# Delta-rule stage: the first level's mask, moved from Pool to the vector engine

## What is computed

```
kb = kc * bc[..., None]
a_mat = jnp.where(tril_strict, jnp.einsum('bhnid,bhnjd->bhnij', kb, kc) * decay, 0.0)
l_mat = a_mat + jnp.eye(CHUNK, dtype=a_mat.dtype)
u = lax.linalg.triangular_solve(l_mat, vc * bc[..., None], left_side=True, lower=True, unit_diagonal=True)
w = lax.linalg.triangular_solve(l_mat, kb * jnp.exp(gc)[..., None], left_side=True, lower=True, unit_diagonal=True)
...
def step(state, inp):
    a_i, qd_i, kt_i, u_i, w_i, gl_i = inp
    v_new = u_i - jnp.einsum('bhck,bhkv->bhcv', w_i, state)
    o_i = jnp.einsum('bhck,bhkv->bhcv', qd_i, state) + jnp.einsum('bhij,bhjv->bhiv', a_i, v_new)
    state = state * gl_i[..., None, None] + jnp.einsum('bhck,bhcv->bhkv', kt_i, v_new)
    return state, o_i
```

## Time and profile before

| | |
|---|---|
| median of 3 runs | 1487.34 us (1486.9 to 1489.47) |
| the profiled execution's own time | 1485.48 us |
| its span | 1483.6 us |
| mean granted TensorE clock | 0.997 |
| busy: PE | 1438.0 us (97%) |
| busy: DVE | 801.7 us (54%) |
| busy: ACT | 619.0 us (42%) |
| busy: Pool | 425.0 us (29%) |
| delta stage | about 1119 to 1245 us of the span |

### The profile page before, as it was taken

One profiled execution on the slowest core, in us unless ns is written; L12 is line 12 of the kernel. 1 busy time (PEld: TensorE's weight loads), 2 busy tenths in 40 slices (PEclk: granted clock), 3 DMA queues, 4 the chain that ended last, 5 costly groups with the idle time before them and its releaser, 6 DMA issues.

```text
span 1483.6 us, 30802 instructions
## 1 busy us (share of the span) xinstructions
PE 1438.0 (97%) x12682; PEld 1267.8 (85%) x12682; DVE 801.7 (54%) x1474; ACT 619.0 (42%) x1249; POOL 425.0 (29%) x527
## 2 busy tenths in 40 slices
PE   6999999989999999999999999999998998999998
PEld 6999998867777778878899999888897886888887
DVE  5238410149999878735420723452424776888431
ACT  5322121027777677632432113332325554777210
POOL 0212132110000277623202212221205884434320
PEclk9999999999999999999999999999999999999999
DMA  8313222000000043256325244433121021222342
GB/s 261 55 51 104 87 92 70 27 1 1 1 1 1 17 130 105 66 177 171 92 43 59 50 94 85 59 59 56 29 68 41 28 90 44 61 76 71 100 131 82
DMA packets 88017, 105.32 MB, mean 71 GB/s; under 512 B 25343, under 2 KB 72095, under 8 KB 87880
## 3 DMA queue, kind: packets, MB, share of 16 engines
q1 hardware_dynamic: 87880, 103.36, 27.0%
HBM read 80.20 MB, written 23.12 MB: 70 GB/s over the span
## 4 chain that ended last, share of the span: by engine, by line
PE 56%; DVE 4%; ACT 2%; DMA 1%; issue 1%; SPq 0%; POOL 0%; DVEq 0%; ACTq 0%
PE ps L368 22%; PE ps L1336 12%; PE ps L2810 2%; PE ps L1144 2%; PE ps L1128 2%; PE ps L2796 2%; PE ps L2785 1%; PE ps L2215 1%; PE ps L2158 1%; PE ps L2173 1%; DMA p_w_raw<-w_in 1%; PE ps L2773 1%; PE ps L1123 1%; PE ps L1122 1%; PE ps L2786 1%
## 5 line engine op out<-in xcount | busy, mean ns | idle before, releaser
L334 POOL TENSOR_TENSOR p_w_lo<-p_w_raw,p_w_hi 128x2048 fp32r<-128x2048 f32 (+1 forms) x27 | 127.3, 4716 | 506.9 <-ACT p_w_hi L318 506.9
L368 PE MATMUL ps<-p_w_hi,w_out_hi 128*128 128x256 f32 (+1 forms) x640 | 181.9, 284 | 0.4 <-ACT p_spill L393 0.3
L368 PE MATMUL ps<-p_w_hi,w_out_lo 128*128 128x256 f32 (+1 forms) x640 | 179.7, 281 | 0.0
L368 PE MATMUL ps<-p_w_lo,w_out_hi 128*128 128x256 f32 (+1 forms) x640 | 179.6, 281 | 0.0
L368 PE MATMUL ps<-p_w_hi,hT_hi 128*128 128x256 f32 x576 | 163.7, 284 | 1.9 <-DVE hT_lo L140 1.9
L368 PE MATMUL ps<-p_w_hi,hT_lo 128*128 128x256 f32 x576 | 162.7, 282 | 0.0
L368 PE MATMUL ps<-p_w_lo,hT_hi 128*128 128x256 f32 x576 | 162.6, 282 | 0.0
L368 PEld LDWEIGHTS ps<-p_w_hi,w_out_hi 128*128 128x128 f32 x640 | 120.5, 188 | 1.5 <-ACT p_spill L393 0.8
L368 PEld LDWEIGHTS ps<-p_w_lo,w_out_hi 128*128 128x128 f32 x640 | 120.8, 189 | 0.0
L368 PEld LDWEIGHTS ps<-p_w_hi,w_out_lo 128*128 128x128 f32 x640 | 120.6, 188 | 0.0
L368 PEld LDWEIGHTS ps<-p_w_hi,hT_hi 128*128 128x128 f32 x576 | 109.0, 189 | 2.3 <-DVE hT_lo L140 2.3
(11 more groups left out here) (299 smaller groups left out, 3585.0 us busy)
## 6 DMA issues: line engine op xcount, KB each, us to landing
p_w_raw<-w_in SPq DMA_DIRECT2D x26, 1024.0 KB, 8.0
s_gate<-p_spill SPq DMA_DIRECT2D x48, 128.0 KB, 1.8
kbT<-x SPq DMA_DIRECT2D x8, 512.0 KB, 6.9
b_w_raw<-w_out SPq DMA_DIRECT2D x8, 512.0 KB, 6.2
qT<-s_gate SPq DMA_DIRECT2D x8, 512.0 KB, 6.9
qT<-x SPq DMA_DIRECT2D x8, 512.0 KB, 3.5
s_x<-qT SPq DMA_DIRECT2D x8, 512.0 KB, 3.1
c_table<-s_line SPq DMA_DIRECT2D x8, 512.0 KB, 3.6
```

The lines of the kernel that those rows point to most:

```text
L334: ops.tensor_tensor(self.w_lo[:, c % 2, :, 0:w], self.raw[:, :, 0:w], self.w_hi[:, c % 2, :, 0:w].bitcast(F32), ALU.subtract).then_inc(sel ...
L368: last = self.nc.tensor.matmul(out, lhs, rhs, start=(kt == 0 and i == 0), stop=(kt == KT - 1 and i == 2))
```

## The change

DVE now multiplies A with the mask of level 0 itself, straight into T, waits for that result, and subtracts T from the identity in place. Pool's mask of level 0 falls away and with it a wait on `T0_ready`. `level_masked` now counts five masks a tile and `T0_ready` two steps a tile, and the waits are renumbered. `Al` keeps its size, its level 0 is no longer written.

```
@@ -2151,7 +2151,7 @@
                 pe.wait_ge(s["X0_ready"], t + 1)
                 if l >= 2:
                     pe.wait_ge(s["X_ready"], m)
-                pe.wait_ge(s["level_masked"], LEVELS * t + l + 1)
+                pe.wait_ge(s["level_masked"], (LEVELS - 1) * t + l)
@@ -2297,17 +2297,20 @@
                 if t >= 1:
-                    dve.wait_ge(s["level_masked"], LEVELS * t)
+                    dve.wait_ge(s["level_masked"], (LEVELS - 1) * t)
                 nc.vector.tensor_tensor(A[:, :, :], own(2), dec[:, 0, :, :], ALU.mult).then_inc(s["A_ready"], 1)
 
             @staticmethod
             def attn(t):
-                dve.wait_ge(s["level_masked"], LEVELS * t + 1)
+                dve.wait_ge(s["A_ready"], t + 1)
+                nc.vector.tensor_tensor(T[:, t % 2, :, :], A[:, :, :],
+                                        levels[:, 0, :].unsqueeze(1).to_broadcast([P, H4, CHUNK]), ALU.mult).then_inc(s["T0_ready"], 1)
+                dve.wait_ge(s["T0_ready"], 2 * t + 1)
                 nc.vector.tensor_tensor(T[:, t % 2, :, :], levels[:, LEVELS + 1, :].unsqueeze(1).to_broadcast([P, H4, CHUNK]),
-                                        Al[:, t % 2, 0, :, :], ALU.subtract).then_inc(s["T0_ready"], 1)
+                                        T[:, t % 2, :, :], ALU.subtract).then_inc(s["T0_ready"], 1)
                 if t >= 2:
                     dve.wait_ge(s["uw_ready"], 2 * (t - 1))
-                dve.wait_ge(s["T0_ready"], t + 1)
+                dve.wait_ge(s["T0_ready"], 2 * t + 2)
                 nc.vector.transpose(blocks(X[:, t % 2]), blocks(T[:, t % 2])).then_inc(s["X0_ready"], 1)
@@ -2545,8 +2548,6 @@
                 pool.wait_ge(s["A_ready"], t + 1)
                 if t >= 2:
                     pool.wait_ge(s["Z_ready"], (LEVELS - 1) * (t - 1))
-                    pool.wait_ge(s["T0_ready"], t - 1)
-                mask_levels(t, 0, 1)
```

## The result

| | before | after |
|---|---|---|
| median (6 runs each) | 1487.59 us | 1493.57 us |
| range | 1486.63 to 1489.47 | 1492.34 to 1496.1 |
| ratio | | 1.0036, 95% interval 1.0026 to 1.0047 |
| span of the profiled execution | 1483.6 us | 1490.0 us |
| profiled execution's own time | 1485.48 us | 1492.34 us |

What follows compares the result with a forecast made beforehand. DVE's queue, not PE, was taken to bound a 4.2 us piece of each settled turn. 5.3 + 0.5 - 0.1 = +5.7 us on 1485.48 gave 1491.2, plus 1.9 for the median: 1493.0 us, range 1489.8 to 1496.1.

Steps and rivals of the forecast that it cites:

- six settled turns: Delta stage, turns three to eight: one more DVE operation beside Pool's masks adds 0.88 us a turn, +5.3 us.
- second turn: Delta stage, second turn: 0.9 us for the added operation, of which 0.42 is covered by DVE's slack, leaving +0.5 us.
- first turn: Delta stage, first turn: DVE multiplies itself instead of waiting for Pool's mask, -0.1 us, bounds -0.8 and +0.3.
- DVE goes first: First turn: DVE's multiply starts ahead of Pool's mask of level 1, so X starts 0.4 us sooner.
- later rise: First turns: TensorE's clock returns to its higher level later, costing up to 1.7 us; left out of the sum.
- Pool's eight masks: Delta stage, Pool: eight masks of 0.69 us fall away, 5.5 us, none on the settled chain, taken at nothing.
- Behind the stage: From 1300 us on: PE is busy for 98 of 100 us, so the delay passes through to the end.
- A: Delta stage: the new pair runs without blocking by Pool, about +2.9 us, 1490.2, a turn of 15.1; chance 0.13.
- B: Delta stage: each engine waits until the other's operation has ended completely, +1.29 us a turn, +8.1 in all, 1495.4; chance 0.10.
- C: Settled turns: X of level 5 really waits for PE, so the change is hidden there, 1487.7 us; chance 0.07.
- D: Delta stage: both new DVE operations find reading free of Pool, time falls by 2.9 us to 1484.4; chance 0.04.
- Two statements on PE: Settled turns: PE busy for 14.31 of 14.59 us, its few idle tenths in DVE's piece; the same busy microseconds after the change.

Runs made afterwards that it cites:

- half-and-half runs: Changed kernel with Pool still making its unread level-0 mask: 1494.11 us; changed kernel with one DVE operation in the pair's place: 1487.07 us.
- runs with Pool held back: Changed kernel, with Pool's masks of levels 2 to 5 waiting until DVE's multiply and subtraction are done: 1488.37 us.
- PSUM run: Changed kernel, with both DVE operations reading the attention product in PSUM and one mask in SBUF, Pool untouched, good for time only: 1488.3 us.
- four faster variants: Changed kernel, multiply straight behind A, without/with masks held back; kernel before, T kept free of Pool, or made by Pool: 1486.46, 1486.43, 1486.82, 1486.79 us.
- early multiply: Changed kernel with DVE's multiply moved up to straight behind A: 1486.46 us.

## Why the prediction was right

The sign and the mechanism were as forecast, +5.7 against +6.0 us measured; part of that closeness is luck, as shown below. Term by term, in the two profiled executions:

- *The six settled turns* were forecast at +5.3, bounds +3.0 and +6.2. From L2184 of the second turn to that of the eighth the trace before shows 1140.37 to 1227.92, the one after 1141.54 to 1234.30, which is +5.21. The single steps came as laid out: the multiply kept T's length (0.79), the subtraction took 0.83 where about 0.79 had been put, but began 0.04 us behind the multiply's end and not 0.11. The two small errors nearly cancel, and X followed 1.77 us behind the multiply, forecast at 1.79 (1181.51 to 1183.3). The half-and-half runs show that this is DVE's side alone.
- *The second turn* was forecast at +0.5. L2184 stood 1.17 us later than before at its end, and the X of level 2, early in it, 0.72 later (1132.72 and 1133.44), so +0.45. X of level 5 followed attnT by 0.31 us, as written, instead of waiting for PE.
- *The first turn* was forecast at -0.1, the mean of branches between which nothing had decided. The branch "DVE goes first" came true, and the 0.4 us it was priced at: X stood 2.22 us behind A's start before and 1.79 after, -0.43. The next turn kept 0.33 of it: a product on PE (L2100) took 0.69 us before and 0.83 now, with the granted clock still at its lower level for its first part (a mean of 0.82 from 1132 to 1133, which puts the rise at about 1132.4; before, at about 1131.4).

```profile
1131.95 0.83 PE L2100 MATMUL ps<-ident,vT 128*128 128x128 f32 x4
```

  So the later rise that the forecast kept for its range did come, 0.9 us later where the work around it stood 0.6 later, but it cost about 0.1 us and not up to 1.7. Between the three branches nothing had decided, and that the sum's -0.1 lay near the -0.33 is chance.
- *Pool's eight masks* were taken at nothing, and in the settled turns they give nothing.
- *Behind the stage* the delay passes through whole: 6.38 us at the last L2184 of the eighth turn (1227.92 and 1234.30), 6.4 at the end of the span.

The stage sums to 5.21 + 0.45 - 0.33 = 5.3 us. The remaining 1.05 us of the span's 6.4 lay between the two executions already before the stage: A of the first turn starts at 1123.88 in one and 1124.93 in the other, though nothing ahead of it was changed. Medians of six runs leave 6.0, and their interval, 3.9 to 7.0 us, holds both 5.3 and 6.4. The agreement of 5.7 and 6.0 is thus partly chance; that of the turns is not.

The rivals: *A*, no blocking, is what the runs with Pool held back and with PSUM inputs look like, and not the changed kernel. Its price was wrong. It put a turn at 15.1, one free operation more than today's blocked T, but when the pair is free, T's own blocking goes too: the two runs show 14.64, only 0.05 above the kernel before, and times that can't be told from it, where A had +2.9 us. (Its terms as written also add up to 2.8, not 2.9.) So A could not have been told from C by the time of a turn. *B*, full blocking, would have put X 2.2 us behind the multiply; it was 1.77. A blocked DVE operation ends 0.28 us behind Pool's, less than the 0.38 to 0.42 that it takes when free, and costs Pool 0.18, not its own length. That its first tenth of a microsecond or so runs beside Pool's operation is my reading of these lengths; no row shows it. So the rule of the Trainium skill (page "SBUF — State Buffer", section "Who interferes with whom") holds here in who blocks whom, as the PSUM run shows, but a price worked out from "fully blocks" comes out too high for operations this short. *C* was wrong, since six turns grew. *D* was wrong for the changed kernel, yet its idea, free reading, is what three of the four faster variants use; the fourth takes the operation off DVE.

Two statements on PE were off. It was to be busy for the same microseconds; it was busy for 14.75 us a turn and not 14.31. And 14.31 of 14.59 us busy seemed to leave 0.28 of idle time, which looks like the 0.27 that freeing DVE gives back. It is not the same quantity: in the four faster variants PE is busy for 14.17 of 14.32 us, and in the changed kernel for 14.75 of 15.46. What DVE's piece is worth is read from the wait of L2184, not from busy time.

## What to carry to other kernels

Price an added operation by what its engine's queue holds at that place and by which other engine it meets there: this one cost 0.87 us in a piece that belonged to DVE, beside Pool's run of masks, and nothing in a gap three operations earlier. Work taken from an engine that ends in a wait anyway is no payment for it. Where two-input DVE operations and Pool operations on SBUF share a stretch, keep them apart by order, a wait, or a PSUM input; then ask which engine is next, since all four ways of freeing DVE stopped at 0.27 us a turn.

## What the runs showed of the hardware

- A DVE operation of 128x256 floats with both inputs in SBUF took 0.38 to 0.43 us alone and 0.79 to 0.83 (0.93 once, in the first turn before) beside a run of Pool's array operations of 0.73 us; with one input in PSUM it took 0.38 to 0.42 either way. Where DVE was the one held up, each meeting made Pool's run 0.18 us longer: 2.79, 2.97, 3.15, 3.33 us for none to three. Where DVE was ahead, Pool's operation took 0.22 to 0.24 longer (0.96 for 0.73, 1.28 for 1.04, 3.01 for 2.79).
- When both wait for the same DVE result, DVE's next operation starts first: 0.04 us behind A's end against 0.09 for Pool (1125.39 and 1125.44, A ending at 1125.35). The early multiply shows the same 0.05 us between them (1180.46 and 1180.51). In both places DVE's operation ran at its free length. No run made Pool go first, so the other branch has no measured price.
